# The scale halves of the modulation matrix move to GpSimd's DMA queue

## The reference, cut to what matters

```python
mod_x = jax.nn.silu(c) @ w_ada[l] + b_ada[l]          # (1, 6144)
sh_x, sc_x, gt_x = jnp.split(mod_x[:, None, :], 3, axis=-1)
mod_c = jax.nn.silu(c_ctx) @ w_ada[l] + b_ada[l]
h_x = _rmsnorm(x, g_pre[l]) * (1 + sc_x) + sh_x
h_c = _rmsnorm(ctx, g_pre[l]) * (1 + sc_c) + sh_c
parts_x = _split_proj(h_x @ w_in[l])                  # 14336 columns
u_c = h_c @ w_in[l][:, U_OFF:U_OFF + W_SSM]
```

## Time and profile before

| | |
|---|---|
| time, median of 3 runs | 2133.92 us (2129.71 to 2136.82) |
| the profiled execution, its own time | 2136.64 us |
| its span | 2134.8 us |
| PE busy | 2068.6 us (97%) |
| DVE busy | 1086.1 us (51%) |
| ACT busy | 585.8 us (27%) |
| POOL busy | 27.1 us (1%) |

### The profile page before, as it was taken

The page is one execution under the profiler, slowest core; times in us unless marked ns, Lnnn a source line. Parts: engine busy times, 40 slices in busy tenths (PEclk is TensorE's granted clock), DMA queues, the critical chain, the costliest instruction groups (busy, mean ns, idle before and its releaser), DMA issues.

```text
span 2134.8 us, 26477 instructions
## 1 busy us (share of the span) xinstructions
PE 2068.6 (97%) x9931; PEld 1674.1 (78%) x9931; DVE 1086.1 (51%) x1596; ACT 585.8 (27%) x816; POOL 27.1 (1%) x16
## 2 busy tenths in 40 slices
PE   3999999999999999999999999999999999999996
PEld 0578888888888888888888888887588888887785
DVE  5445889888888545544333444322433333332233
ACT  4325333333333322222222222222122222221221
POOL 0003100000000000000000000000000000000000
PEclk9999999999999999999999999999999999999998
DMA  9863533333334544443334444434033333332423
GB/s 371 312 207 121 161 99 103 104 91 102 99 103 111 166 135 124 129 145 101 92 106 140 131 131 130 139 111 133 20 94 93 99 99 98 94 94 98 165 93 117
DMA packets 384546, 270.08 MB, mean 127 GB/s; under 512 B 24774, under 2 KB 349870, under 8 KB 382886
## 3 DMA queue, kind: packets, MB, share of 16 engines
q1 hardware_dynamic: 374132, 264.95, 40.4%
q10 hardware_dynamic: 10356, 4.35, 1.5%
HBM read 251.17 MB, written 18.09 MB: 126 GB/s over the span
## 4 chain that ended last, share of the span: by engine, by line
PE 81%; DVE 9%; DMA 4%; ACT 2%; ACTq 2%; issue 2%; SPq 0%; DVEq 0%
PE ac L704 20%; PE ac L705 20%; PE ac L708 20%; ACTq L1097 2%; DVE S L1556 2%; DMA M<-Tl 1%; PE ac L878 1%; PE ac L879 1%; PE ac L880 1%; PE ss L880 1%; PE ss L878 1%; PE ss L879 1%; DMA wslot<-w_in 1%; ACT S L901 1%; PE ac L845 1%
## 5 line engine op out<-in xcount | busy, mean ns | idle before, releaser
L1455 DVE TENSOR_TENSOR wlo<-wslot,whi 128x1024 fp32r<-128x1024 f32 x310 | 379.4, 1224 | 655.6 <-ACT whi L901 651.4
L901 ACT ACTIVATE whi<-wslot 128x1024 fp32r<-128x1024 f32 x328 | 347.0, 1060 | 1269.2 <-PE ac L708 1032.6
L704 PE MATMUL ac<-hxh,whi 128*128 128x512 f32 x1664 | 652.3, 392 | 0.1
L705 PE MATMUL ac<-hxl,whi 128*128 128x512 f32 x1664 | 647.9, 389 | 0.0
L708 PE MATMUL ac<-hxh,wlo 128*128 128x512 f32 x1664 | 411.1, 389 | 0.9 <-DVE wlo L1455 0.9
L704 PEld LDWEIGHTS ac<-hxh,whi 128*128 128x128 f32 x1664 | 312.4, 188 | 68.4 <-issue 3.1
L708 PEld LDWEIGHTS ac<-hxh,wlo 128*128 128x128 f32 x1664 | 312.3, 188 | 66.1 <-DVE wlo L1455 1.3
L705 PEld LDWEIGHTS ac<-hxl,whi 128*128 128x128 f32 x1664 | 312.4, 188 | 64.1 <-issue 0.2
L704 PE MATMUL ac<-bah,whi 128*128 128x512 f32 x384 | 149.4, 389 | 0.0
L705 PE MATMUL ac<-bal,whi 128*128 128x512 f32 x384 | 149.4, 389 | 0.0
L708 PE MATMUL ac<-bah,wlo 128*128 128x512 f32 x384 | 94.8, 389 | 0.0
(11 more groups left out here) (320 smaller groups left out, 2153.7 us busy)
## 6 DMA issues: line engine op xcount, KB each, us to landing
wslot<-w_in SPq DMA_DIRECT2D x224, 512.0 KB, 3.9
ring<-w_ada SPq DMA_DIRECT2D x64, 512.0 KB, 7.9
gwt<-w_ada SPq DMA_DIRECT2D x128, 128.0 KB, 2.4
wslot<-w_out SPq DMA_DIRECT2D x32, 512.0 KB, 3.5
wslot<-proj_a SPq DMA_DIRECT2D x16, 512.0 KB, 4.0
wslot<-proj_b SPq DMA_DIRECT2D x16, 512.0 KB, 4.1
wslot<-proj_c SPq DMA_DIRECT2D x16, 512.0 KB, 4.0
xn<-x SPq DMA_DIRECT2D x4, 1024.0 KB, 8.7
```

Source lines behind the costliest of these rows:

```text
L704: mm(ac[:, bank, :], w, xh, start=(v == 0 and q == 0), stop=False)
L705: mm(ac[:, bank, :], w, xl, start=False, stop=False)
L901: cp = lambda o, i, scale=1.0: nc.scalar.activation(o, i, ACT.Copy, scale=scale)
L1455: tt(wlo[:, s, :], wslot[:, s, :], whi[:, (U0[k] + j) % 2, :].bitcast(F32), ALU.subtract)\
```

## The change

The scale half of each block gets a semaphore set of its own, `ada_sc`, and is issued by GpSimd, which runs over the 32 blocks with the same waits for the slot. SP keeps the shift half and its other loads in their order. TensorE waits for both semaphores ahead of a block. GpSimd's ten subtractions stand behind its 32 DMAs.

```diff
+    ada_sc = [sem(f"ada_sc{i}") for i in range(4)]
...
-            for h in range(2):
-                sp.dma_start(ring[n % 4][:, :, h, :],
-                             w_ada[r * 256:(r + 1) * 256, h * D + q * 512:h * D + (q + 1) * 512]
-                             .rearrange("(k p) c -> p k c", p=128)).then_inc(ada_in[n % 4], 16)
+            sp.dma_start(ring[n % 4][:, :, 0, :],
+                         w_ada[r * 256:(r + 1) * 256, q * 512:(q + 1) * 512]
+                         .rearrange("(k p) c -> p k c", p=128)).then_inc(ada_in[n % 4], 16)
...
+        for n in range(32):
+            q, r = n // 8, n % 8
+            if n >= 4:
+                pool.wait_ge(ada_used, n - 3)
+            pool.dma_start(ring[n % 4][:, :, 1, :],
+                           w_ada[r * 256:(r + 1) * 256, D + q * 512:D + (q + 1) * 512]
+                           .rearrange("(k p) c -> p k c", p=128)).then_inc(ada_sc[n % 4], 16)
         pool.wait_ge(w_lo, UFIRST)
...
-            pe.wait_ge(ada_in[n % 4], 32 * (n // 4 + 1))
+            pe.wait_ge(ada_in[n % 4], 16 * (n // 4 + 1))
+            pe.wait_ge(ada_sc[n % 4], 16 * (n // 4 + 1))
```

## The result

Twenty runs of the changed kernel have a median of 2142.14 us (2137.00 to 2145.46), twenty of the kernel before 2136.25 us (2128.67 to 2138.31). The ratio is 1.0031, with a 95% interval of 1.0023 to 1.0040: slower by 4.9 to 8.5 us, forecast +7.1. The profiled execution has a span of 2141.1 us against 2134.8, +6.3 us.

What follows compares the result with a forecast made beforehand. It took the first stage to be bound by DVE's chain behind the small load `ldt`. The terms 5.1 + 1 + 0 + 0.5 + 0.5 gave +7.1 us, a median of 2141.0 us, range 2131 to 2152.

Steps and rivals of the forecast that it cites:

- The bound, and the time to spare: Up to 50 us, DVE's chain behind the small load `ldt` is the bound; the w_ada blocks have 6.4 us to spare.
- The blocks after the change: Start of the kernel: blocks 4 to 7 end within some 2 us of 41.43, and their cover grows to 9 us.
- (1): Start: GpSimd's first four scale halves go ahead of `ldt` as a third queue; +5.1 us, between 0 and 5.4.
- (2): DVE's chain before 50 us: GpSimd's eight DMA issues hold up DVE steps; +1 us, between 0 and 3.8.
- Rival C: DVE's chain is held up more, by 3.8 to 7.6 us: 2144 to 2148 us; chance 0.18.
- (3): SP's queue: 32 issues of 0.47 us go, but SP is never late; value 0.
- (4): Ring refills from 56 to 138 us: nothing gained or lost below 2.7 us per GpSimd issue; taken as +0.5 us.
- The sign of being wrong: After 56 us: waits for the ring of more than 5 us would show the forecast wrong.
- rival B: Refills: GpSimd's issues take over 2.7 us, at 4 us each 22 us in all: 2156 us; chance 0.1.
- (5): TensorE after 56 us: one more wait ahead of each of 24 blocks, some 0.02 us each; +0.5 us.
- Rival A: Start and refills: GpSimd's packets don't precede ACT's, refills gain at most 3.1 us: 2131; chance 0.22 together with D.
- D: All DMA queues: they only interleave on the same 16 engines, no effect: 2134 us; chance 0.22 together with Rival A.

Runs made afterwards that it cites:

- e3: Changed kernel, but GpSimd waits for ACT's small loads before its first DMA; ratio 1.0006 to the kernel before.
- e1: Changed kernel, but GpSimd issues only the scale halves of blocks 0 to 3, SP the rest; ratio 1.0016 to the kernel before.
- e2: Changed kernel, but SP issues both halves of blocks 0 to 3, GpSimd scale halves from block 4 on; ratio 1.0005 to the kernel before.
- e6: Changed kernel, but GpSimd issues only the scale halves of blocks 0 and 1, SP the rest; ratio 1.0010 to the kernel before.
- e11: Changed kernel, but SP and GpSimd hold back each next group until the last block has landed in full; ratio 1.0030 to the kernel before.
- e8_before_again: The kernel before, unchanged, run for a second profile; the stage from first to last columns takes 88.6 us, 87.8 in the first profile.
- e10: Changed kernel, but each scale half is issued as two DMAs of 128 rows; ratio 1.0035 to the kernel before.

## Why the prediction was right

*The bound, and the time to spare.* Right. The stretch to 50 us looked like a bound by DMA and was DVE's chain behind a load of 0.5 KB. e3 delayed block 7 to 47.61 us and cost nothing.

*The blocks after the change.* Wrong, without harm. "Nothing after is late" and a cover of 9 us left out that a slot comes free only after `cs`, which hangs on the late small loads. Block 7 was late by 5.3 us and not within 2, the cover stayed at 6.0, and the gap before the transpose was 7.3 us and not 12. DVE's chain was still last, so the sum did not feel it; with 6 us more on the blocks it would have.

*(1) The third queue beside ACT's, +5.1 us.* Right in mechanism and size: +5.2. e1 alone brings it, e2 and e3 alone take it away, e6 halves it. One detail was wrong, the packets: GpSimd's hold two rows, 512 packets for the four halves and not 1024. The ceiling by bytes, 5.4 us, did not depend on it.

*(2) DVE's chain beside GpSimd's descriptors, +1 us.* Right in mechanism, too large: 31.90 against 31.72 us, 0.2 us, because only one of the eight issues caught a one-source step in that part of it. The most in any run is 0.9 us, with four issues in a row. The rule of the Trainium skill, "SBUF — State Buffer", section "Who interferes with whom", agrees with the steps of 0.37 to 0.45 us in e11, and in the direction that the prediction priced: the issue is there first, and DVE waits. The earlier trace rows could not show that, since the DVE instruction there has two sources. Rival C (3.8 to 7.6 us) is out: no issue cost DVE more than 0.26 us.

*(3) SP's issues: 0.* Nothing in the runs speaks against it.

*(4) The refills, +0.5 us.* Too small. The stage took 2.5 us more in this pair of profiles; 0.9 of it is within the spread of the unchanged kernel, about 0.8 go with GpSimd's refills, and the rest is not explained. The sign of being wrong, ring waits of over 5 us, came up (7.3), but it was a poor one: the unchanged kernel shows 5.7 in its second profile. The bound by GpSimd's issue time, 2.7 us, was never near, at 0.72: rival B is out.

*(5) The second wait, +0.5 us.* Not to be seen: TensorE's unexplained gaps before these blocks are 9.2 us in 29 of them before and after.

So (2) and (5) were too high and (4) too low, each by 0.5 to 2 us, and that they nearly cancel is luck; against the sum of 7.1 the runs have 5.9 at the medians and 4.9 to 8.5 by the interval. It is luck, too, that 2141.0 lies so near the median of 2142.14: the kernel before came out 2.3 us above the three runs that the prediction started from. "Nothing gives the delay back" was wrong in one profile for a reason outside the change: a clock drop in the profile of before. Rival A is out by the time of GpSimd's first packets: 54 of them lie before 8 us. For D, the Trainium skill, "DMA: Bandwidth & Descriptors", section "Issuing engines are not separate DMA queues", agrees with the turns of 146, 146 and 145 in that the DMAs interleave. But D's "no effect" is out, since the small loads of a third engine paid for it.

## What to carry to other kernels

Before a load is moved to another queue, ask which small loads are in flight in that stretch, count their packets, and see who waits for them. Here each of their packets waited for about one packet of every other busy queue, so they paid by the size of those packets, and all that the new queue had at the start went ahead. Ask also what the small loads hold up behind them: here they held the ring's slots, and the big blocks came 5.3 us later though their bytes were the same. The cheap cure is the reverse: keep the packets in front of latency-bound loads small (here 2 KB for 8 KB in the first 4 MB, -0.22%), or hold the new queue back until those loads have landed (e3: no change of the time is shown).

## What the runs showed that I had not expected

- DMAs from GpSimd's queue moved two rows of 2 KB in one packet of 4 KB, SP's one row; with one row of each partition a DMA the packets were still of 4 KB (e10).
- An issue of GpSimd's made a one-source DVE step of 0.20 us last up to 0.45 us, and left the two-source steps at 0.23 us (e11).
- An issue on GpSimd took 0.72 us, on SP 0.37 at the median of the same kernel, and GpSimd's first packet of the second refill came 2.8 us after the block's slot was free (2.3 in e2).
- The time of one kernel moves by some 10 us from run to run (2128.67 to 2138.31), and part of it seems to be TensorE's clock. The granted clock from 1950 to 2000 us, where the engine works without a gap, is 0.86 in the profile of before and 0.97 in e8_before_again, the same kernel, whose span is 5.8 us shorter. The spans of single profiles here can therefore differ by as much as the effect under study. Single steps near the start differ far less (0.3 us for `ldt` in four profiles), and twenty runs of each kernel tell 0.3% apart.
